# Who rounds five row tiles of w_out: GpSimd around one root, or ScalarE between its exponentials

## The reference, cut to what matters

```python
def mixer(h, w_in, w_out, lam, lam_init, subln_g, sinks):
    proj = jnp.einsum('bsd,de->bse', h, w_in)
    ...
    oa = diff_attention(...)        # 4 heads, "A", each with its own rmsnorm
    ob = moba_attention(...)        # 6 heads, "B"
    oc = swa_sink_attention(...)    # 6 heads, "C"
    o = jnp.concatenate([oa.reshape(B, S, A_V_W), ob.reshape(B, S, B_W), oc.reshape(B, S, C_Q_W)], axis=-1)
    return jnp.einsum('bse,ed->bsd', o, w_out)
```

## Time and profile before

| what | value |
|---|---|
| median of 3 runs | 1521.2 us (1520.54 to 1522.17) |
| the profiled execution's own time | 1523.7 us |
| its span in the trace | 1521.9 us |
| mean granted clock of TensorE | 0.996 of full speed |
| busy: TensorE, VectorE, ScalarE, GpSimd | 98%, 83%, 47%, 41% |
| where the change lies | 205 to 230 us of the span |

### The profile page before, as it was taken

How to read it: one execution, slowest core, us unless ns; L and a number is a source line. 1 busy time by engine, 2 the same in 40 slices (tenths; PEclk the granted TensorE clock), 3 DMA queues, 4 the chain that set the end, 5 groups by cost and what they waited for, 6 DMA issues and landing times.

```text
span 1521.9 us, 24327 instructions
## 1 busy us (share of the span) xinstructions
PE 1485.8 (98%) x8276; PEld 1325.0 (87%) x8276; DVE 1270.7 (83%) x2491; ACT 713.5 (47%) x1411; POOL 621.2 (41%) x511
## 2 busy tenths in 40 slices
PE   5999999999999999999999999999999999999998
PEld 4887777888999999999989999999999988888886
DVE  6788665689999989898678888888999988888876
ACT  4444553233345747576554344444444444443344
POOL 1121300033461424253356555556767655555301
PEclk9999999999999999999999999999999999999999
DMA  9854320122355879899999999999999999999962
GB/s 360 296 175 155 144 79 1 40 100 90 106 186 181 281 230 297 276 300 301 318 362 378 354 359 355 364 339 369 396 385 389 369 371 411 383 380 391 346 243 104
DMA packets 164147, 417.14 MB, mean 274 GB/s; under 512 B 12745, under 2 KB 70217, under 8 KB 163921
## 3 DMA queue, kind: packets, MB, share of 16 engines
q1 hardware_dynamic: 95984, 244.88, 45.1%
q0 software_dynamic: 41472, 151.01, 26.3%
q10 hardware_dynamic: 26594, 20.05, 4.1%
HBM read 376.57 MB, written 38.80 MB: 273 GB/s over the span
## 4 chain that ended last, share of the span: by engine, by line
PE 79%; DVE 13%; DMA 3%; issue 1%; SPq 1%; ACT 1%; POOL 0%; ACTq 0%; DVEq 0%; POOLq 0%
PE bank_S L1092 17%; PE bank_O L1030 14%; PE bank_T L1092 11%; PE bank_S L1030 9%; PE bank_G L1092 6%; PE bank_T L1070 5%; PE bank_O L773 2%; DMA u_raw<-in_u_t 2%; PE bank_S L740 2%; DVE mod_acc L2294 2%; DVE mod_acc L2264 2%; DVE v_sb L2270 1%; DVE v_sb L2257 1%; DVE si L2276 1%; DVE si L2263 1%
## 5 line engine op out<-in xcount | busy, mean ns | idle before, releaser
L1725 ACT ACTIVATE v_hi<-v_raw 128x1024 fp32r<-128x1024 f32 x124 | 131.5, 1061 | 284.6 <-PE bank_G L1092 272.2
L1694 ACT ACTIVATE u_hi<-u_raw 128x1024 fp32r<-128x1024 f32 x128 | 135.4, 1058 | 207.8 <-PE bank_O L1030 104.9
L2575 DVE TENSOR_TENSOR v_lo<-v_raw,v_hi 128x1024 fp32r<-128x1024 f32 x124 | 152.1, 1227 | 86.6 <-ACT v_hi L1725 63.4
L1430 POOL DMA_INDIRECT row<-in_peer_v,stage x128 | 176.4, 1378 | 42.2 <-issue 38.1
L1030 PE MATMUL bank_S<-h_hi,u_hi 128*128 128x352 f32 x576 | 191.7, 335 | 1.4 <-ACT a_act L1745 1.3
L1430 POOL DMA_INDIRECT row<-in_peer_u,stage x128 | 145.4, 1136 | 103.9 <-POOL stage L1426 98.2
L1030 PE MATMUL bank_S<-h_lo,u_hi 128*128 128x352 f32 x576 | 184.9, 323 | 0.0
L2565 DVE SCALAR_TENSOR_TENSOR y<-row,wgt,y 128x1024 f32<-128x1024 f32 x128 | 164.2, 1283 | 0.0
L2591 DVE SCALAR_TENSOR_TENSOR row<-row,h 128x1024 f32<-128x1024 f32 x128 | 156.2, 1221 | 0.0
L1030 PE MATMUL bank_O<-h_lo,u_hi 128*128 128x352 f32 x448 | 144.7, 325 | 0.0
L1030 PE MATMUL bank_O<-h_hi,u_hi 128*128 128x352 f32 x448 | 143.8, 322 | 0.0
(11 more groups left out here) (450 smaller groups left out, 3773.1 us busy)
## 6 DMA issues: line engine op xcount, KB each, us to landing
u_raw<-in_u_t SPq DMA_DIRECT2D x128, 512.0 KB
v_raw<-in_peer_v SPq DMA_DIRECT2D x128, 512.0 KB
g_in<-gates SPq DMA_DIRECT2D x32, 768.0 KB
ada_late<-in_w_ada SPq DMA_DIRECT2D x8, 2048.0 KB, 8.4
gates<-g_out SPq DMA_DIRECT2D x8, 2048.0 KB, 10.1
spill<-a_act ACTq DMA_DIRECT2D x64, 176.0 KB
a_act<-spill SPq DMA_DIRECT2D x16, 704.0 KB
w_raw<-in_w_in SPq DMA_DIRECT2D x20, 512.0 KB, 4.0
```

The source lines that it names most:

```text
L1430: pool.indirect_dma_start(rows[slot][:, :], None, table[:, :], bass.IndirectOffsetOnAxis(stage[:, place:place + 1], 0))\
L1694: act.activation(u_hi[c % 2][:, :], u_raw[:, c % 2, :], ACT.Copy).then_inc(s_uhi, 1)
L1725: act.activation(v_hi_end[:, i % TAIL, :] if end else v_hi[:, c % 2, :], v_raw[c % 4][:, :], ACT.Copy)\
L2575: dve.tensor_tensor(lo[:, q, :], v_raw[c % 4][:, :], hi[:, q, :].bitcast(f32), ALU.subtract)\
```

## The change

The five high parts of tiles 0 to 4 leave ScalarE's list and stand in GpSimd's, two ahead of the root and three behind it. GpSimd's first copy waits until all five loads have landed, until the last projection of w_in is done (its inputs lie where the copies go) and until ScalarE has made the three high parts that it keeps, so that the count `s_wohi` keeps its order. The copy of tile 4 waits for the last A group's product, as before. VectorE's table is renamed `LOW_AT` and unchanged in content.

```diff
-        OUT_AT = {34: 6, 35: 7, 39: 5, 41: 0, 42: 1, 43: 2, 44: 3, 45: 4}
+        LOW_AT = {34: 6, 35: 7, 39: 5, 41: 0, 42: 1, 43: 2, 44: 3, 45: 4}
+        OUT_AT = {J: k for J, k in LOW_AT.items() if k > 4}
...
+            def out_high(k):
+                if k == 4:
+                    taken(pool, ("o", 2 * NT - 1))
+                pool.tensor_copy(out_hi(k), in_pieces(k, w_outs[k][:, :])).then_inc(s_wohi, 1)
+
+            pool.wait_ge(s_wout, 16 * 5)
+            unit_done(pool, 19)
+            pool.wait_ge(s_wohi, 3)
+            for k in (0, 1):
+                out_high(k)
             pool.wait_ge(s_zero, 4)
             pool.wait_ge(s_sso, 1)
             pool.tensor_tensor(sso[:, :], sso[:, :], power[:, :], ALU.pow).then_inc(s_so, 1)
+            for k in (2, 3, 4):
+                out_high(k)
...
-                if k > 4:
-                    act.wait_ge(s_wout_c, 16 * (3 if k == 5 else 2))
-                    act.wait_ge(s_accd, 12)
-                else:
-                    act.wait_ge(s_wout, 16 * 5)
-                    unit_done(act, 19)
-                if k == 4:
-                    taken(act, ("o", 2 * NT - 1))
-                raw = w_outs[k][:, :]
-                act.activation(out_hi(k), in_pieces(k, raw), ACT.Copy).then_inc(s_wohi, 1)
+                act.wait_ge(s_wout_c, 16 * (3 if k == 5 else 2))
+                act.wait_ge(s_accd, 12)
+                act.activation(out_hi(k), in_pieces(k, w_outs[k][:, :]), ACT.Copy).then_inc(s_wohi, 1)
...
-                if J - 1 in OUT_AT:
-                    out_low(OUT_AT[J - 1])
+                if J - 1 in LOW_AT:
+                    out_low(LOW_AT[J - 1])
```

## The result

| | before | after |
|---|---|---|
| median of 22 runs each, side by side | 1521.92 us (1520.16 to 1525.48) | 1523.97 us (1522.63 to 1528.97) |
| ratio after to before, 95% interval | | 1.0017 [1.0010, 1.0023] |
| the profiled execution's own time | 1523.7 us | 1525.54 us |
| its span | 1521.9 us | 1523.7 us |
| mean granted clock of TensorE | 0.996 | 0.995 |

The change costs 0.17%, some 2.6 us by the ratio, with 1.5 to 3.5 us as its interval; the two medians lie 2.05 us apart. The time lies in the predicted range of 1519.8 to 1525.0 us. The forecast had the sign right and about half of the size: 1.2 us.

A forecast was written before the change was run, and what follows sets the result against it. TensorE bounds the kernel, with VectorE's chain setting the end of its hole at 222 to 226 us. Terms 0 + 0.57 + 0.89 - 0.3 = +1.2 us give 1522.4 us; range 1519.8 to 1525.0.

The forecast's parts named there:

- Relief: Removing five ScalarE copies gains 0, since VectorE sets the end of TensorE's hole at 222 to 226 us; upper bound 1.6.
- One copy: Price of one high-part copy on GpSimd: 1.04 us, from the slope of the one-input select.
- Place one: At J = 40, GpSimd's first copy delays tile 5's low part and TensorE's first projection pass: +0.57 us.
- Place two: At J = 44 and 45, GpSimd's fifth copy delays tile 2's or tile 3's low part on the chain: +0.89 us.
- The clock: Low-clock stretch behind the hole starts 0.57 later, so more of it lies inside the longer hole: -0.3 us.
- The sum: Whole kernel: 0 + 0.57 + 0.89 - 0.3 = +1.2 us, making 1522.4 us on the median of 1521.2.
- VectorE goes undisturbed: Rival: copies do not delay VectorE's low parts, so both delay terms vanish: 1521.2 us; chance 0.15.
- The clock stays up: Rival: TensorE's granted clock does not fall behind the hole, 1.46 - 1.7 = -0.2: 1521.0 us; chance 0.15.
- Loop pace: Rival: a GpSimd copy takes 1.5 us, stretching the delays of tile 5's and later low parts: 1524.4 us; chance 0.11.
- subtraction pace: Rival: a GpSimd copy takes 2.396 us like its subtraction, delaying low parts and root, +7.7: 1528.9 us; chance 0.06.

The follow-up runs named there:

- e4: Changed kernel with no high-part copies of tiles 0 to 4, products using tile 5's instead (wrong results); 1522.24 us, ratio to before 1.0001.
- e3: Changed kernel, but tile 4's high part stays on ScalarE and GpSimd's first copy waits for tile 5's low part; 1522.09 us, ratio to before 1.0000.
- e6: Kernel before plus two spare memsets on GpSimd where the change puts its first two copies; 1521.89 us, ratio to before 1.0000.
- e5: Kernel before plus two spare copies on GpSimd where the change puts its first two; 1521.2 us, ratio to before 0.9995.
- e2: Changed kernel, but GpSimd's first copy also waits for tile 5's low part; 1524.39 us, ratio to before 1.0014.
- e1: Changed kernel, but tile 4's high part stays on ScalarE, leaving GpSimd four copies; 1521.6 us, ratio to before 0.9998.
- e9: Changed kernel with VectorE's low parts of tiles 3 and 4 and first norm step put behind `soft_in` of jobs 48 and 49; 1524.26 us, ratio to before 1.0013.
- second traces: Kernel before and changed kernel, both unedited, each profiled once more; 1522.09 and 1523.09 us.
- e8: Kernel before with low parts of tiles 3 and 4, their ScalarE high parts and the first norm step moved later; 1522.59 us, ratio to before 1.0002.
- e11: Kernel before, low parts of tiles 2 and 3 pulled into VectorE's idle time, tile 4 and first norm step later; second timing, 1519.59 us, ratio 0.9982.

## Why the prediction was right, and where it was off

**Relief, predicted 0: shown.** e4 gives all of it and its stretch equals e3's and e6's to 0.01 us. The prediction read it from the chain against the list of waits, and that reading held: the wait list named ScalarE for 1.4 of 1.6 us, and all 1.6 were VectorE's once ScalarE was out of the way. Nor did the relief keep the clock up: it was 1.00 in e4, but also in e5 and e6, where ScalarE makes all five copies.

**One copy, predicted 1.04 us: shown,** 1.04 in after, in e2 and in e5. The slope of the one-input select carried over to a copy to the hundredth.

**Place one, predicted +0.57: shown, +0.59.** It is there in the scores too (14.75 and 14.79 against 14.17). The first pass goes from 2.69 to 3.28 in each kernel that has a copy there (after, e1, e5, e9) and in none that has not (e2, e3, e4, e6). The stretched instruction, predicted at about 1.8, is 1.81.

**Place two, predicted +0.89: shown in the instruction, +0.88 to 0.89** (2.10 or 2.11 less 1.22), in after, e2 and e9. It was tile 2's low part that lost a turn, not tile 3's. That the chain carries it to TensorE in full is shown by the scores of e2, which has this term alone: 15.05 against 14.18 before, +0.87, at a clock of 1.00 up to there. With both terms after has 15.67, +1.49, where the prediction had the hole end 1.46 later. That the delay then stays to the end of the stretch is an inference, 40.04 = 37.32 + 0.59 + 0.89 + what the clock took: no kernel with this term had both the order of after and a clock of 1.00 throughout.

**The clock, predicted -0.3: wrong in sign, +0.3 in the profiled pair.** This is the step that was mis-sized. In before, the low clock takes 38.26 - 37.32 = 0.94 us of the stretch, in after 40.04 - 37.32 - 0.59 - 0.89 = 1.24. The second traces give 0.76 and 1.05, the same difference. The prediction let the low stretch begin 0.57 later, tied to the beginning of the hole, so that more of it would lie inside. It did not: the four scores behind the hole took 1.09 us in before but 0.70 in after, still at full speed, and the low clock came some 2 us behind them (0.91 from 228 to 230, 0.50 from 230 to 232; before had 0.54 from 226 to 228), in work that has nothing to wait for. What was lost is the same in both, 4 x (0.04 + 0.38) = 1.7 us of full-speed work in after. Why it came later is open. That 4 x 0.43 = 1.7 us of lost full-speed work costs only 0.94 in before has in part a cause in the rows: at full speed TensorE waits 0.3 and 0.2 us for VectorE soon after (e3's last two rows of waits), and at the lower level these waits are not there, so about 0.5 of the 1.7 falls into idle time; the last 0.3 is not explained. In after only the first of the two is gone.

**The sum.** 0.59 + 0.89 + 0.3 = 1.8 us, which is what the profiled pair shows in the stretch (1.78) and in the span (1.8). The medians say 2.05, and the ratio 2.6, with 1.5 at its lower end. Later markers of the same pair (first `wq` product at 299 us, first `u_hi` product at 402, first `v_hi` product at 780) give +1.77, +1.78 and +1.71, so no other place in that pair adds to it. Most of what the ratio has above 1.8 sits in three of the 22 executions of after (1527.71, 1527.75 and 1528.97 us), the only ones whose mean clock was 0.994. With them the mean of after is 2.5 us above that of before, without them 2.0. So more was lost to the clock there, but where, and whether the change has a part in it, is open: of 15 runs of before timed later one took 1527.96 us, also at 0.994. The forecast of 1522.4 us also stood on the median of three runs, 1521.2; that of 22 is 0.7 higher.

**The rivals.** "VectorE goes undisturbed" fell with 1.81 and 2.10. "The clock stays up" fell in both traces of after, but it is what happened in e5, e6, e3, e4 and e1, with a hole of 1.6 us; that it fell in both of after may be luck, since nothing found here says when it does. "Loop pace" and "subtraction pace" fell with 1.04. The chance of 0.84 for within 0.2% was too sure: the interval of the ratio reaches 1.0023, and the two terms of 1.5 us with an unlucky clock come close to the bound of 3.04.

## What to carry to other kernels

When work moves to GpSimd, first list VectorE's instructions with two SBUF operands that would start beside it and ask who waits for each: beside a copy on GpSimd such an instruction loses what is left of that copy (up to 0.89 of 1.04 us here), and an "idle" GpSimd is then not free. A wait list that names one engine may hide a second that is due at nearly the same time; the chain shows it, and a kernel that leaves the suspected work out proves it (e4). A hole that is set by an engine's amount of work moves when part of it is put off (e8) and shrinks, here from 2.1 to 0.9 us, when work is pulled into that engine's idle time ahead of it (e11, ratio 0.9982 [0.9973, 0.9991]).

## What the runs showed of the hardware that was not expected

- The root (power, 128x16, 2.95 us on GpSimd, inputs in SBUF) does not hold up VectorE's two-operand instructions: 2.35 us for two beside it, in every trace, as for two with nothing beside them (2.36 in e4). A copy of 1.04 us does. Why the one blocks and the other does not is open.
- Of a copy and a low part the one that was issued first went first, and the other stood still. In e5 the low part (issued at 211.87) went ahead of the second copy (212.54, which then took 2.04 us); in after the third copy (220.32) waited for the tail of tile 1's low part and took 1.35. They need not alternate: the fourth and fifth copies of after ran back to back, the fifth issued at 222.61 and tile 2's low part at 222.62.
- An instruction with one SBUF operand can be held up as well: the scaled sums (TENSOR_SCALAR, 128x16) took 0.44 us beside the second copy in e2 and in e3, and 0.17 in before. A reduction (128x256) beside the same copy in e2 kept its 0.42.
- The granted clock fell behind the hole in some executions and not in others. In e5 and e6 TensorE's waits are those of before (1.4 and 0.2 us), and the clock was 1.00 from 226 to 234 us where both traces of before had 0.57. In e9 it stayed at 1.00 behind 2.39 us of idle time and in e8 it fell behind 2.00. Nothing that the rows show of the hole itself sorts the two groups; what does is open.
